# Squares of the late tiles on ScalarE, in their own PSUM banks, and their sums on VectorE one tile later

## The chip, the cores and the metric

The kernel runs on one core of a Trainium2 chip. Such a core has five engines that work side by side, each through its own queue in a fixed order: TensorE (PE in the rows; its weight loads are PEld) multiplies matrices into PSUM, VectorE (DVE), ScalarE (ACT) and GpSimd (POOL) work element by element, and SyncE (SP) issues most DMA transfers. Engines wait for one another only through semaphores. The metric is the device time in microseconds (us) of one execution of the whole program; lower is better. TensorE's clock is granted by the chip at one of two levels, 2.4 or 1.2 GHz; the profile shows it as 1.0 or 0.5.

## The reference, cut to what matters

Two layers of a diffusion backbone on 512 latent tokens, with 256 context tokens beside them in the first layer. The model width is 1024.

```
for i in range(2):
    h = modulate(rmsnorm(x, g_mix_pre), shift, scale)
    y = token_mixer(h) @ w_out                     # "output product"
    x = x + gate * rmsnorm(y, g_mix_post)          # "residual"
    h = modulate(rmsnorm(x, g_ffn_pre), shift, scale)
    a, u = split(h @ w_ffn_in)
    y = (silu(a) * u) @ w_ffn_out                  # "hidden product"
    x = x + gate * rmsnorm(y, g_ffn_post)
```

`rmsnorm(y, g)` is `y * rsqrt(mean(y*y) + eps) * g`, with the mean over the 1024 features of a token. So after each product y the kernel needs the sum of the squares of all eight tiles of y before it can form a residual, and then the sum of squares of the new x before it can form the next h.

## The kernel before, in words

**Layout and stages.** Everything is stored feature-major: 128 features on the partitions, 8 tiles of features (`KT`), tokens along the free axis. An output tile m is a chain of matmuls over 8 feature tiles (6 for the last block of the hidden product). Each fp32 product is made of three reduced-precision matmuls (weight high x activation high, high x low, low x high), so a tile takes 24 (or 18) matmuls. Weights stream from memory in chunks: SyncE loads a chunk into `raw` (two places), ScalarE rounds it to `w_hi` (line 1304), GpSimd forms `w_lo` (line 913), and TensorE uses it from a ring of four places (`RING`). A load waits until GpSimd is done with the chunk two before it; a rounding waits until TensorE has used the chunk four before it.

**The order.** `build_order` writes out by hand one list of units of work, `ORDER`. Every engine walks through the same list and issues its own share of each unit, so the list fixes each queue.

**The transitions.** Between a product y and the next stage lies a transition, written by `tail(L, w)`: L is the layer, w = 0 after the output product and w = 1 after the hidden product. There are four. The tokens are cut into two parts: in layer 0 columns 0 to 511 (latent) and 512 to 767 (context), in layer 1 two halves of 256. Product tiles of the first part are done before the transition. In it, TensorE makes the second part's tiles, the eight units `late(m)` for m = 0 to 7, each of 256 columns, in bank 1 of the PSUM tensor `A[m % 2]`, while the first part goes through `mean` (a matmul with 1/1024 that sums the squares over partitions; line 1268), `res` (residual, VectorE, lines 2052 and 2053 or 2060 and 2061), `sq` (squares of x on ScalarE, line 1613, summed by TensorE, line 1277), `rstd` (ScalarE, lines 1317 to 1321) and `nrm` (norm and modulation: VectorE line 2071, ScalarE lines 1621, 1624, 1627, VectorE line 2078 for four of the eight tiles and GpSimd line 958 for the others). Between the late tiles stand `modk` units, products for the next modulation (line 995); SyncE loads a later piece of their weights only when an earlier one has been used, and weight chunks queue behind that load.

The order of a transition in layer 0: late 0, mean 0, late 1, take 0, res 0 and 1, take 1; then four times late(2+i), ahead(1+i), squares of x, a modulation product, two residuals (not the fourth time), take(2+i); then rstd, late 6, ahead 5, nrm 0 to 2, late 7, ahead 6, take 6, nrm 3 to 7, ahead 7, take 7, head 0 of the first part, mean 1 of the second part, then the second part's res, sq, rstd and nrm. Layer 1's first transition is alike. Its last one has no squares of x and no norms: late(2+i), two residuals, take(2+i), and at the end late 6, take 6, late 7, take 7, mean 1.

**`take(m)`** evicts late tile m (VectorE, lines 1972 to 1989). With w = 0 it copies the tile to y, squares it into a spare bank of `N` and adds the square to the running sum `ssq`; with w = 1, y already holds the sum of the earlier blocks, so it adds the tile to y, squares and adds. The semaphore `free[A0]` or `free[A1]` goes up when the second of these instructions (the first with w = 1) is done; `late(m+2)` waits for it at `unit_free`.

**`head(L, w, 0, 0)`** is the first tile of the next stage's product for the first part. It is made in A0: before its first matmul TensorE waits until all earlier users of A0, late(6) among them, have been evicted (lines 1027 to 1032), then before each of the eight k-steps for the normalised tile k. `mean(L, w, 1)` stands behind it in TensorE's queue.

**`ahead(j)`** is a weight rounding on ScalarE (`high`), and `link` makes an engine wait for its own last instruction.

Of the kernel before, what the change touches and what calls it, by code (L numbers as in the profile page):

```python
# [12 lines left out]
ACT = mybir.ActivationFunctionType  # L13

P = 128
DEPTH, D, SEQ, CTX = 2, 1024, 512, 256
# [311 lines left out]
def sums_before(L, w):  # L328

    return KT * (4 * L + 2 * w)  # L330
# [88 lines left out]
LOW_V = (0, 3, 5, 7)  # L419
SQ, NRM, RES = ({e: i + 1 for i, e in enumerate(x for x in ORDER if x[0] == kind)} for kind in ("sq", "nrm", "res"))  # L420
# [62 lines left out]
def bass_hybrid_block(nc: bass.Bass, stream, pairs, modw, xT, pos_row, pos_col, cols, wdec, masks, mats, wide, x_keep, out):  # L483
    with ExitStack() as ctx:
# [3 lines left out]
        def sem(name):  # L488
            return ctx.enter_context(nc.semaphore(name))
# [134 lines left out]
        haff_ready, hhi_ready = sem("haff_ready"), sem("hhi_ready")  # L624
        yn_ready, rstd_copied, half_done = sem("yn_ready"), sem("rstd_copied"), sem("half_done")
# [67 lines left out]
        def rstd_at(e):  # L693

            t0, t1, _ = span(e)
            return sum_bank(e) if e in IN_PSUM else rstd[:, t0:t1]

# [266 lines left out]
        def _(pe):  # L964
# [35 lines left out]
            for e in ORDER:  # L1000
# [263 lines left out]
                elif kind == "mean":  # L1264
                    unit_free(e)
                    t0, t1, _ = span(e)
                    pe.wait_ge(ssq_ready, sums_before(L, e[2]) + KT * (e[3] + 1))
# [13 lines left out]
        def _(act):  # L1281
# [112 lines left out]
            for e in ORDER:  # L1394
# [200 lines left out]
                elif kind == "ahead":  # L1595
                    high(TWICE[0] + KT + e[3] if L else PLAN.n0[("late",) + e[1:]] + RING)
                elif kind == "mean":
# [51 lines left out]
        def _(dve):  # L1649
# [131 lines left out]
            for e in ORDER:  # L1781
# [190 lines left out]
                elif kind == "take":  # L1972
                    w, m = e[2:]
                    t0, t1, _ = parts(e)[1]
                    late = ("late", L, w, m)
                    at = t0 + L * SEQ // 2
                    ym, src = y[:, m, t0:t1], A[m % 2][:, at:at + t1 - t0]
                    dve.wait_ge(chunk_used, (TWICE[w] + m if L else PLAN.n0[late]) + 1)
                    square = N[:, 512:512 + t1 - t0]
                    if w:  # L1980
                        dve.tensor_tensor(ym, src, ym, ALU.add).then_inc(free[f"A{m % 2}"], 1)
                        read_out(dve, late)
                        link(dve.tensor_tensor(square, ym, ym, ALU.mult))
                    else:
                        link(dve.tensor_copy(ym, src))
                        dve.tensor_tensor(square, src, ym, ALU.mult).then_inc(free[f"A{m % 2}"], 1)
                        read_out(dve, late)
                    dve.wait_ge(ssq_ready, sums_before(L, w) + KT + m)
                    dve.tensor_tensor(ssq[:, t0:t1], square, ssq[:, t0:t1], ALU.add).then_inc(ssq_ready, 1)
# [220 lines left out]
```

## Time and profile before

| | |
|---|---|
| device time, median of 3 runs | 1675.63 us (1671.38 to 1683.51) |
| profiled execution | 1675.34 us, span 1673.5 us |
| busy in the span | TensorE 95%, VectorE 44%, ScalarE 34%, GpSimd 36% |
| mean granted clock | 0.988 |
| DMA | 111 GB/s mean |
| first transition (about 386 to 446 us) | TensorE busy 54.8 of 60 us |
| second (940 to 1012) | 59.6 of 72 |
| third (1244 to 1312) | 59.9 of 68 |
| last (1643 to 1673.5) | 19.1 of 30.5 |

A line "L975 PE MATMUL A<-h_hi,w_hi" names the line of the kernel, the engine, the operation, the tile written and the tiles read (buffer numbers left out). Times of a timeline count from the start of the span. The bracket at the end of a row says how long the engine had been idle and whose work ended that wait.

### The profile page before, as it was taken

To read this page: it belongs to the slowest core of one execution; us is meant where nothing else is said; L and a number is where in the kernel's file an instruction comes from. 1 tells how busy PE (TensorE), PEld (TensorE's weight loads), DVE (VectorE), ACT (ScalarE), POOL (GpSimd) and SP (SyncE) were. 2 spreads that over 40 slices of the span, in tenths; PEclk is the share of its full clock that TensorE was granted. 3 is DMA by queue.
4 is the path that set the end of the run, shared out by engine and by line. 5 is a ranking of instruction groups with operands and counts; after the bars stand their busy time and mean duration, and the time that the engine had idled before them with its cause. 6 is when DMAs were issued, how large, how long until landed. Compare 5 with 4: busy or idle time off the path is not lost.

```text
span 1673.5 us, 23315 instructions
## 1 busy us (share of the span) xinstructions
PE 1596.0 (95%) x9320; PEld 1347.2 (81%) x9320; DVE 728.7 (44%) x1208; ACT 573.7 (34%) x924; POOL 603.2 (36%) x317
## 2 busy tenths in 40 slices
PE   5999999999899999999999989999989999999997
PEld 2778877877689989998998657887886888888887
DVE  2400325845666425761465554045754321221137
ACT  4534213524634313441243345432523422222221
POOL 1422211334424425553255433232132444444442
PEclk9999999999999999999999999999999999999999
DMA  9444332154312112222123653211071222222221
GB/s 374 160 160 151 124 107 80 39 201 176 151 39 93 72 38 83 69 77 75 51 76 117 261 195 107 66 67 59 28 277 51 79 97 100 89 100 92 97 87 64
DMA packets 50210, 185.25 MB, mean 111 GB/s; under 512 B 5254, under 2 KB 10246, under 8 KB 43208
## 3 DMA queue, kind: packets, MB, share of 16 engines
q1 hardware_dynamic: 44028, 170.29, 28.1%
q10 hardware_dynamic: 6092, 13.70, 2.2%
q8 instruction: 64, 1.05, 0.2%
q14 instruction: 26, 0.21, 0.0%
HBM read 172.44 MB, written 11.53 MB: 110 GB/s over the span
## 4 chain that ended last, share of the span: by engine, by line
PE 81%; DVE 5%; issue 4%; DMA 3%; ACT 3%; POOL 3%; SPq 1%; ACTq 0%; DVEq 0%; POOLq 0%
PE A L975 55%; PE A L1221 7%; PE N L1221 4%; PE G L1221 4%; DMA raw<-stream 2%; POOL w_lo L913 2%; PE G L1277 1%; DMA raw<-modw 1%; PE N L995 1%; PE G L995 1%; PE A L1117 1%; PE G L1083 1%; PE G L1051 1%; PE N L1067 1%; PE G L1124 1%
## 5 line engine op out<-in xcount | busy, mean ns | idle before, releaser
L913 POOL TENSOR_TENSOR w_lo<-raw,w_hi 128x1024 fp32r<-128x1024 f32 (+2 forms) x175 | 403.2, 2307 | 729.1 <-ACT w_hi L1304 692.3
L975 PE MATMUL A<-h_hi,w_hi 128*128 128x512 f32 (+1 forms) x1264 | 416.4, 360 | 21.8 <-POOL h_lo L958 12.7
L975 PE MATMUL A<-h_hi,w_lo 128*128 128x512 f32 (+1 forms) x1264 | 407.1, 353 | 0.0
L975 PE MATMUL A<-h_lo,w_hi 128*128 128x512 f32 (+1 forms) x1264 | 406.5, 352 | 0.0
L1304 ACT ACTIVATE w_hi<-raw 128x1024 fp32r<-128x1024 f32 (+2 forms) x175 | 177.2, 1015 | 429.2 <-PE A L975 362.5
L975 PEld LDWEIGHTS A<-h_hi,w_hi 128*128 128x128 f32 x1264 | 223.4, 190 | 80.7 <-POOL h_lo L958 18.8
L975 PEld LDWEIGHTS A<-h_hi,w_lo 128*128 128x128 f32 x1264 | 224.1, 191 | 33.0
L975 PEld LDWEIGHTS A<-h_lo,w_hi 128*128 128x128 f32 x1264 | 223.8, 191 | 31.9 <-issue 0.5
L975 PE MATMUL A<-g_hi,w_hi 128*128 128x512 f32 (+1 forms) x528 | 165.2, 352 | 3.8 <-DVE g_lo L1778 2.0
L975 PE MATMUL A<-g_lo,w_hi 128*128 128x512 f32 (+1 forms) x528 | 162.9, 348 | 0.0
L975 PE MATMUL A<-g_hi,w_lo 128*128 128x512 f32 (+1 forms) x528 | 162.9, 348 | 0.0
L953 POOL TENSOR_TENSOR w_lo<-w_sum,w_hi 128x512 fp32r<-128x512 f32 x45 | 81.0, 1824 | 146.4 <-DVE w_sum L1705 100.0
L1836 DVE TENSOR_TENSOR eu<-eu,ktok 128x256 f32<-128x256 f32 x24 | 34.4, 1434 | 186.0 <-ACT dec L1450 185.9
L975 PEld LDWEIGHTS A<-g_hi,w_hi 128*128 128x128 f32 x528 | 90.9, 189 | 23.4 <-issue 5.2
L975 PEld LDWEIGHTS A<-g_lo,w_hi 128*128 128x128 f32 x528 | 90.6, 188 | 15.0 <-issue 1.0
L975 PEld LDWEIGHTS A<-g_hi,w_lo 128*128 128x128 f32 x528 | 90.7, 188 | 14.1
L1337 ACT ACTIVATE w_hi<-w_sum 128x512 fp32r<-128x512 f32 x81 | 49.2, 625 | 120.8 <-DVE w_sum L1705 120.8
L2029 DVE TENSOR_TENSOR sqb<-sqb,A 128x512 f32<-128x512 f32 x22 | 15.1, 688 | 147.5 <-PE A L975 147.5
L2032 DVE TENSOR_TENSOR g_lo<-sqb,g_hi 128x512 f32 (+1 forms) x22 | 50.7, 2305 | 24.0 <-ACT g_hi L1567 24.0
L958 POOL TENSOR_TENSOR h_lo<-y,h_hi 128x256 fp32r<-128x256 f32 (+1 forms) x32 | 31.5, 989 | 78.8 <-ACT h_hi L1624 78.4
L1277 PE MATMUL G<-sqs,one_d 128*128 128x512 f32 (+1 forms) x80 | 35.3, 571 | 22.0 <-ACT sqs L1613 21.8
L953 POOL TENSOR_TENSOR w_lo<-raw,w_hi 128x512 fp32r<-128x512 f32 x27 | 39.0, 1458 | 31.0 <-ACT w_hi L1337 31.0
(294 smaller groups left out, 2494.0 us busy)
## 6 DMA issues: line engine op xcount, KB each, us to landing
raw<-stream SPq DMA_DIRECT2D x150, 512.0 KB, 3.2
mraw<-modw SPq DMA_DIRECT2D x38, 1024.0 KB, 5.0
raw<-pairs SPq DMA_DIRECT2D x18, 512.0 KB, 4.6
raw<-stream SPq DMA_DIRECT2D x24, 384.0 KB, 2.9
raw<-modw SPq DMA_DIRECT2D x6, 1024.0 KB, 14.7
x<-x_keep ACTq DMA_DIRECT2D x4, 1536.0 KB, 11.0
mraw<-pairs SPq DMA_DIRECT2D x9, 512.0 KB, 3.2
x_keep<-x SPq DMA_DIRECT2D x4, 768.0 KB, 21.6
```

The source lines that it names most:

```text
L913: pool.tensor_tensor(lo, like_chunk(n, raw[:, n % RAW, 0:WIDTH[n]]), hi.bitcast(F32), ALU.subtract).then_inc(lo_done, 1)
L953: pool.tensor_tensor(lo, src, f_weight(w_hi, q, pos).bitcast(F32), ALU.subtract).then_inc(f_lo, 1)
L958: pool.tensor_tensor(h_lo[:, k, t0:t1], y[:, k, t0:t1], h_hi[:, k, t0:t1].bitcast(F32), ALU.subtract).then_inc(hlo_ready_p, 1)
L975: m = pe.matmul(dst[:, t0:t1], a, b[:, k, t0:t1], start=(first and p == 0), stop=(last and p == 2))
L995: mm = pe.matmul(dst[32 * j:32 * j + 32, 0:512], csil[:, k, :], piece_at(p)[:, 512 * j:512 * j + 512], start=(k == 0), stop=(k == KT - 1))
L1051: pe.matmul(unit_of(e), lrT[0:33, tt * P:(tt + 1) * P], wd[:, :], start=True, stop=True).then_inc(full["z"], 1)
L1221: m = pe.matmul(dst, a[:, cols], b[:, k, :], start=(k == 0 and p == 0), stop=(k == 3 and p == 2))
L1277: pe.matmul(sum_bank(e), one_d[:, :], sq_at(e), start=(k == 0), stop=(k == KT - 1)).then_inc(sq_used, 1)
L1304: act.activation(w_hi[:, n % RING, 0:width], src, ACT.Copy).then_inc(hi_done, 1)
L1337: act.activation(f_weight(w_hi, q, pos), src, ACT.Copy).then_inc(f_hi, 1)
L1836: dve.tensor_tensor(eu[:, g, :], eu[:, g, :], ktok[:, tt, :], ALU.mult).then_inc(ku_ready, 1)
L2032: dve.tensor_tensor(g_lo[:, gp, 0:T], sqb[:, 0:1, 0:T], g_hi[:, gp, 0:T].bitcast(F32), ALU.subtract).then_inc(g_ready, 1)
```

## The change

ScalarE now has a share in every `take`. With w = 0 it copies the late tile from PSUM to y, waits for that, and squares the tile in place, in its PSUM bank. With w = 1 VectorE still adds the tile to y, and ScalarE then writes the square of y into the tile's PSUM bank. VectorE adds a square to `ssq` one unit later: in take(m) it adds the square of tile m-1 straight from the bank, in take(7) those of 6 and 7. Only that addition raises `free[A0]` or `free[A1]`. The second part's `mean` waits for the releases of tiles 6 and 7. The order list is unchanged.

```diff
--- before.py
+++ after.py
@@ -327,7 +327,7 @@
 
 def sums_before(L, w):
 
-    return KT * (4 * L + 2 * w)
+    return KT * (2 * L + w)
 
 
 def span(e):
@@ -417,6 +417,8 @@
 PIECE = {e: i for i, e in enumerate(PIECES)}
 MTURN = {e: i + 1 for i, e in enumerate(x for x in ORDER if x[0] == "mturn")}
 LOW_V = (0, 3, 5, 7)
+TAKE = {e: i + 1 for i, e in enumerate(x for x in ORDER if x[0] == "take")}
+ADDED = {e: i + 1 for i, e in enumerate(x for x in ORDER if x[0] == "take" and x[2])}
 SQ, NRM, RES = ({e: i + 1 for i, e in enumerate(x for x in ORDER if x[0] == kind)} for kind in ("sq", "nrm", "res"))
 
 YN = {e: i + 1 for i, e in enumerate(x for x in ORDER if x[:4] == ("res", 1, 1, 1) and x[4] % 2)}
@@ -622,6 +624,7 @@
         ssq_ready, rstd_ready, xnew_ready, sq_ready, sq_used = (
             sem("ssq_ready"), sem("rstd_ready"), sem("xnew_ready"), sem("sq_ready"), sem("sq_used"))
         haff_ready, hhi_ready = sem("haff_ready"), sem("hhi_ready")
+        late_added, late_sq = sem("late_added"), sem("late_sq")
         yn_ready, rstd_copied, half_done = sem("yn_ready"), sem("rstd_copied"), sem("half_done")
         hlo_ready_p, hlo_ready_v = sem("hlo_ready_p"), sem("hlo_ready_v")
         pair_in, sums_ready, f_hi, f_lo, f_used = (
@@ -694,6 +697,16 @@
 
             t0, t1, _ = span(e)
             return sum_bank(e) if e in IN_PSUM else rstd[:, t0:t1]
+
+        def late_at(e):
+
+            t0, t1, _ = parts(e)[1]
+            at = t0 + e[1] * SEQ // 2
+            return A[e[3] % 2][:, at:at + t1 - t0]
+
+        def late_done(e):
+
+            return (TWICE[e[2]] + e[3] if e[1] else PLAN.n0[("late",) + e[1:]]) + 1
 
         def sq_at(e):
 
@@ -1264,7 +1277,11 @@
                 elif kind == "mean":
                     unit_free(e)
                     t0, t1, _ = span(e)
-                    pe.wait_ge(ssq_ready, sums_before(L, e[2]) + KT * (e[3] + 1))
+                    if e[3]:
+                        for m in (KT - 2, KT - 1):
+                            read_out(pe, ("late", L, e[2], m))
+                    else:
+                        pe.wait_ge(ssq_ready, sums_before(L, e[2]) + KT)
                     pe.matmul(sum_bank(e), one_d[:, :], ssq[:, t0:t1],
                               start=True, stop=True).then_inc(full["mean"], 1)
                 elif kind == "sq":
@@ -1594,6 +1611,16 @@
                             high(n0 + j + RING, i, width=WIDTH[n0] if e[2] == 2 else None)
                 elif kind == "ahead":
                     high(TWICE[0] + KT + e[3] if L else PLAN.n0[("late",) + e[1:]] + RING)
+                elif kind == "take":
+                    t0, t1, _ = parts(e)[1]
+                    ym = y[:, e[3], t0:t1]
+                    if e[2]:
+                        act.wait_ge(late_added, ADDED[e])
+                        act.activation(late_at(e), ym, ACT.Square).then_inc(late_sq, 1)
+                    else:
+                        act.wait_ge(chunk_used, late_done(e))
+                        link(act.activation(ym, late_at(e), ACT.Copy))
+                        act.activation(late_at(e), ym, ACT.Square).then_inc(late_sq, 1)
                 elif kind == "mean":
                     if e[2] and e[3] == 0:
                         act.preload_act_table_set(LN_SET)
@@ -1972,21 +1999,15 @@
                 elif kind == "take":
                     w, m = e[2:]
                     t0, t1, _ = parts(e)[1]
-                    late = ("late", L, w, m)
-                    at = t0 + L * SEQ // 2
-                    ym, src = y[:, m, t0:t1], A[m % 2][:, at:at + t1 - t0]
-                    dve.wait_ge(chunk_used, (TWICE[w] + m if L else PLAN.n0[late]) + 1)
-                    square = N[:, 512:512 + t1 - t0]
                     if w:
-                        dve.tensor_tensor(ym, src, ym, ALU.add).then_inc(free[f"A{m % 2}"], 1)
-                        read_out(dve, late)
-                        link(dve.tensor_tensor(square, ym, ym, ALU.mult))
-                    else:
-                        link(dve.tensor_copy(ym, src))
-                        dve.tensor_tensor(square, src, ym, ALU.mult).then_inc(free[f"A{m % 2}"], 1)
-                        read_out(dve, late)
-                    dve.wait_ge(ssq_ready, sums_before(L, w) + KT + m)
-                    dve.tensor_tensor(ssq[:, t0:t1], square, ssq[:, t0:t1], ALU.add).then_inc(ssq_ready, 1)
+                        dve.wait_ge(chunk_used, late_done(e))
+                        dve.tensor_tensor(y[:, m, t0:t1], late_at(e), y[:, m, t0:t1], ALU.add).then_inc(late_added, 1)
+                    for j in ((m - 1,) if 0 < m < KT - 1 else (m - 1, m) if m else ()):
+                        of = e[:3] + (j,)
+                        dve.wait_ge(late_sq, TAKE[of])
+                        if j:
+                            read_out(dve, ("late", L, w, j - 1))
+                        dve.tensor_tensor(ssq[:, t0:t1], late_at(of), ssq[:, t0:t1], ALU.add).then_inc(free[f"A{j % 2}"], 1)
                 elif kind == "ffn_in" and L == 0:
                     for q in range(FAST):
                         if q == 3:
```

## Rows read from the trace of the kernel before

**Rows 1.** The page's first part: busy us (share of the span) xinstructions.

```profile
PE 1596.0 (95%) x9320; PEld 1347.2 (81%) x9320; DVE 728.7 (44%) x1208; ACT 573.7 (34%) x924; POOL 603.2 (36%) x317
```

**Rows 2.** Eviction lines: xcount, duration ns min/median/max, first and last start, form.

```profile
L1981 DVE TENSOR_TENSOR y<-A,y x16: 414/416/426, 948.7 to 1662.7; 128x256 f32<-128x256 f32 x16
...
L1985 DVE COPY y<-A x16: 414/422/425, 388.6 to 1287.3; 128x256 f32<-128x256 f32 x16
...
L1986 DVE TENSOR_TENSOR N<-A,y x16: 432/432/433, 389.1 to 1287.7; 128x256 f32<-128x256 f32 x16
...
L1989 DVE TENSOR_TENSOR sqb<-N,sqb x32: 424/424/425, 389.6 to 1663.6; 128x256 f32<-128x256 f32 x32
```

**Rows 3.** TensorE's waits, whole span: us in total, times, longest us.

```profile
PE G L1277 <- ACT sqs L1613: 21.8, 6, 12.4
...
PE N L1268 <- DVE sqb L1989: 2.6, 3, 1.5
...
PE A L975 <- DVE y L1981: 1.2, 2, 0.7
```

**Rows 4.** ScalarE, PSUM to SBUF and to PSUM (columns as rows 2).

```profile
L1319 ACT ACTIVATE rstd<-N,eps x5: 474/474/476, 30.0 to 1004.1; 128x256 f32<-128x256 f32 x5
...
L1321 ACT ACTIVATE N<-N x5: 368/368/582, 390.1 to 1646.6; 128x256 f32<-128x256 f32 x3, 128x512 f32<-128x512 f32 x2
```

**Rows 5.** TensorE's timeline (start, us), first transition: late(2), head, second mean begin.

```profile
392.09 0.28 PE L975 MATMUL A<-h_hi,w_hi 128*128 128x256 f32 x1
...
421.03 0.50 PE L975 MATMUL A<-h_hi,w_hi 128*128 128x512 f32 x1
...
430.74 0.67 PE L1268 MATMUL N<-sqb,one_d 128*128 128x256 f32 x2 [0.41 <-DVE sqb L1989]
```

**Rows 6.** VectorE's timeline, first transition: take(1) and take(7) begin.

```profile
393.58 0.41 DVE L1985 COPY y<-A 128x256 f32<-128x256 f32 x1
...
429.25 0.42 DVE L1985 COPY y<-A 128x256 f32<-128x256 f32 x1
```

**Rows 7.** Chain of waits (start, us, what), first transition: an unstalled head.

```profile
432.41 5.71 PE A L975 x24
```

**Rows 8.** TensorE's timeline, second transition: two square products, and the second mean.

```profile
956.24 1.10 PE L1277 MATMUL G<-sqs,one_d 128*128 128x512 f32 x2 [2.63 <-ACT sqs L1613]
...
959.92 1.99 PE L1277 MATMUL G<-sqs,one_d 128*128 128x512 f32 x4 [0.47 <-ACT sqs L1613]
...
992.51 0.59 PE L1268 MATMUL N<-sqb,one_d 128*128 128x256 f32 x2
```

**Rows 9.** VectorE's timeline, second transition: take(1) and take(7) begin.

```profile
954.87 0.41 DVE L1981 TENSOR_TENSOR y<-A,y 128x256 f32<-128x256 f32 x1
...
989.26 0.42 DVE L1981 TENSOR_TENSOR y<-A,y 128x256 f32<-128x256 f32 x1
```

**Rows 10.** The chain of waits, last transition: late 6 and 7, and the mean.

```profile
1658.05 4.59 PE A L975 x36
...
1664.17 0.68 PE N L1268 x2
```

**Rows 11.** ScalarE's timeline, third transition: a weight rounding, and norm 3.

```profile
1253.66 1.06 ACT L1304 ACTIVATE w_hi<-raw 128x1024 fp32r<-128x1024 f32 x1 [5.98 <-DMA raw<-stream]
...
1283.52 0.48 ACT L1621 ACTIVATE h_hi<-A,coef 128x256 fp32r<-128x256 f32 x1 [0.70 <-DVE A L2071]
```

**Rows 12.** Timeline, third transition: take(7) begins; the second mean.

```profile
1287.30 0.42 DVE L1985 COPY y<-A 128x256 f32<-128x256 f32 x1
...
1288.79 0.67 PE L1268 MATMUL N<-sqb,one_d 128*128 128x256 f32 x2 [0.66 <-DVE sqb L1989]
```

**Rows 13.** VectorE's timeline, last transition: take(1)'s first instruction.

```profile
1648.69 0.41 DVE L1981 TENSOR_TENSOR y<-A,y 128x256 f32<-128x256 f32 x1
```

**Rows 14.** The chain of waits, second transition: the end of the head.

```profile
988.07 4.60 PE A L975 x12
```

**Rows 15.** That stretch: us, busy PE PEld DVE ACT POOL (x), clock, DMA, GB/s.

```profile
988.10:991.60 3.50, 3.50 (x10) 2.72 (x11) 1.96 (x6) 1.50 (x2) 1.15 (x1) 0.59 0.54 152
```

## The prediction, written before the change was run

> **What bounds the kernel now.** The page's busy times come first: TensorE is busy 95% of the span [rows 1], so only its idle time, or new idle time, can move the result. Which idle time touches this change is seen in the waits of TensorE and in the rows of the eviction lines. The 32 late evictions cost VectorE three instructions each, 0.42 to 0.43 us apiece [rows 2], but TensorE waited for them for only 2.6 us before the mean products and 1.2 us at bank releases [rows 3]. About 4 us is all that a quicker eviction could return there. The larger waits (21.8 us for ScalarE's squares of x) belong to a chain that the change does not shorten. The next views are the timelines of the four transitions. The reader should see what TensorE does while the chain residual, square, rstd, norm runs on VectorE and ScalarE: it works on late tiles and then on the next stage's first product ("head"), whose eight steps take each normalised tile as it appears.
>
> **What is removed and added.** In an output-product transition (w = 0) VectorE loses the copy and the square and keeps the addition; ScalarE gets a copy and a square. In a hidden-product transition (w = 1) VectorE keeps y+A and the addition, and ScalarE gets the square. The nearest rows for ScalarE on 256 columns are 0.47 us (Ln, PSUM to SBUF) and 0.37 us (Exp, PSUM to PSUM) [rows 4]. I take 0.47 for the copy and 0.42 for the square, 0.9 for the pair; ends 0.7 and 1.0.
> The Trainium skill's page VectorE: DVE Perf Modes, section on the TRN2 errata, gives ScalarE 172 cycles plus the column count at 1.2 GHz for PSUM to SBUF, so 0.36 us for the copy, an estimate; the sum would be 0.1 us shorter, and rows 4 say it is too low.
>
> **What is moved** is what counts: the release of bank A(m). Before, it followed take(m)'s second instruction (first where w = 1). After, it follows the addition inside take(m+1), and for m = 6 and 7 both inside take(7). All waits for that release stay where they were: late(m+2) on TensorE, and the head, which waits until late(6) has left A0. VectorE's queue order is fixed, so everything that stands there between take(m) and take(m+1) now lies ahead of the release: two residual pairs for late(2), norms 0 to 2 for late(7), norms 3 to 7 for the head. ScalarE's weight roundings, squares of x and norms queue behind its new instructions. SyncE and GpSimd get nothing new; their loads are late only where TensorE's modulation products are, because SyncE waits for those.
>
> *Layer 0, output product.* Late(2) started at 392.09 us, while VectorE finished the residuals only when the old take(1) could start, 393.58 [rows 5, 6]. The addition (0.42) takes that place, so late(2) starts at 394.1: 2.0 us late. TensorE has no slack before the squares of x, so rstd and the norms are 2.0 late. ScalarE, which sets the pace of norms 3 to 7, gets take(6)'s pair between norms 2 and 3: another 0.9. VectorE therefore reaches take(7) at 429.25 + 2.9 = 432.15 instead of 429.25 [rows 6] and releases A0 at 432.6. The head, which began at 421.03 and ran under the norms [rows 5], can start only at 432.7. It needs the 5.71 us that the next, unstalled head of 24 matmuls took [rows 7]: end 438.4. The mean product behind it started at 430.74 [rows 5]: **+7.7 us**. The late(7) stall (it waits for norms 0 to 2) and the last square are hidden inside this wait. All that follows hangs on that mean, so it moves by as much.
>
> *Layer 0, hidden product.* Y+A of take(1) starts at 954.87 [rows 9], the addition ends 0.8 later, and late(2) runs from 955.8 to 958.1 (36 such matmuls took 4.59 us, half of that for 18 [rows 10]). TensorE's first square product started at 956.24, after an idle 2.63, and a later one after an idle 0.47 [rows 8]. So 1.9 us is lost and 0.5 absorbed: 1.4. ScalarE's extra square in take(6): 0.4. VectorE reaches take(7) at 989.26 + 1.8 = 991.1 [rows 9], needs y+A and the addition (0.84), and the head runs from 992.0 to 997.8. The mean started at 992.51 [rows 8]: **+5.3 us**.
>
> *Layer 1, output product.* Late(2) is some 0.5 late (it waits for one residual pair of 256 columns), but the square of x waits for ScalarE, which sits out 5.98 us for a weight load [rows 11]: absorbed, cost nothing; were that load early, it would be 0.5. ScalarE's pair fits in its idle 0.70 but for 0.2 [rows 11]. Take(7) is reached at 1287.30 + 0.2 [rows 12], the release comes 0.42 later, the head takes 24/36 of 4.59 = 3.06 [rows 10] and ends at 1291.1, where the mean started at 1288.79 [rows 12]: **+2.3 us**.
>
> *Layer 1, hidden product.* Here nothing but residuals lies between late tiles. Take(2+i) first waits for late(2+i), then adds, and only then frees the bank for late(3+i): the two banks become one. Each tile costs 2.3 us of matmuls, two VectorE instructions of 0.42 and the hand-overs, 3.2 us together. Late(2) starts 0.9 after take(1) at 1648.69 [rows 13], five more follow, and late(7) ends at 1649.6 + 5 x 3.2 + 2.3 = 1667.9, against 1662.6 before (1658.05 + 4.59) [rows 10]. The last square takes as long as VectorE's did, and VectorE loses one instruction: **+5.0 us** on the mean at 1664.17 [rows 10].
>
> The four make **20.3 us**.
>
> *Clock.* Where TensorE had stood idle inside the second transition's head, the granted clock fell: a mean of 0.59 over 988.10 to 991.60, between the levels 2.4 and 1.2 GHz, and 12 matmuls took 4.60 us [rows 14, 15], against 12/24 of 5.71 = 2.86 [rows 7]: 1.7 us lost. The change puts idle times of 7, 5 and 3 us right ahead of three heads. I charge 1.7 each: **+5.1**. Ends: 0, and seven such losses (12) if the last transition's repeated 0.9 us gaps count too.
>
> **Sum.** 20.3 + 5.1 = 25.4 on the profiled execution's own 1675.34 us (span 1673.5 and 1.8 around it) gives 1700.7. That execution lies 0.3 below the median 1675.63 of the three runs, which spread from 1671.38 to 1683.51. I forecast **1701 us**; its own range is 1694 to 1708.
>
> **Rivals.**
> *Clock worse.* TensorE's own rows after idle time speak for it [rows 14, 15]; against it, part of the lowered stretch falls into the idle time itself. 20.3 + 12 and some: 1709. Chance 0.13.
> *The heads are covered.* If the release on which the head waits came early (norms not ahead of it on VectorE, or ScalarE no longer the pace), only the late(2) stalls and the last transition would stay: 2.0 + 0.9, 1.8, 0.2 and 5.0, about 10: 1686. The fixed order speaks against it. Chance 0.12.
> *Not slower: the freed VectorE decides.* Place: VectorE between rstd and the head. Price: 3.8 us of TensorE's waits [rows 3] and two instructions (0.85) less in the norms of three transitions, 2.5: 6.3 together, so 1669. It decides only if each bank comes free before TensorE asks for it, that is if VectorE passes its norms before late(7) ends; it passed them at 429.25 while the head, behind late(7), began at 421.03 [rows 5, 6]. The Trainium skill's page TensorEngine Tiling (Array Packing), section PSUM Bottleneck, advises using both ScalarE and VectorE to evacuate PSUM; that is this rival, and the time it would give is the one just worked out. Chance 0.06.
> *The change does not spread the work.* ScalarE's takes block its own queue: it waits for late(m), or for VectorE's addition, ahead of the weight roundings. If one weight tile in each of the first three transitions came 3 us late to TensorE, 1701 + 9 = 1710. Roundings run four tiles ahead, which speaks against it. Chance 0.05.
> The forecast keeps 0.64.
>
> **How the numbers follow.** A difference of 1% (17 us) is about what separates a change from none for this kernel. The forecast, the worse clock and the blocked queue lie above it: 0.82, of which I move 0.01 to same for the nearness of 1694. The covered heads and the freed VectorE lie within it, 0.18, of which 0.03 is kept for a faster result than any case explains. Slower 0.81, same 0.16, faster 0.03. The range 1688 to 1712 takes in the clock's lower end (1695.6), a weight load in the second transition that does not shift (1.4 less), the spread of runs, and the upper rivals; 1686 and below stay out.
>
> **What would show it.** In the changed kernel's profile TensorE should have a new wait for VectorE's additions of squares of about 6 us ahead of the first head, 5 ahead of the second and 2 to 3 ahead of the third; waits of 0.9 us five or six times in the last transition; and a late(2) that starts as the second residual ends. VectorE's busy time should fall by about 32 x 0.43 = 14 us and ScalarE's rise by 16 x 0.9 + 16 x 0.4 = 21. Heads that still start under the norms, or late tiles that run back to back in the last transition, would prove the prediction wrong.

## The result, and the profile after

The changed kernel took 1705.11 us (median of 4 runs, 1694.80 to 1709.43) against 1674.68 us before (4 runs, 1671.38 to 1683.51): a ratio on record of 1.0154, interval 1.0125 to 1.0183 (the bare quotient of these two medians is 1.018, at the upper end of it). The forecast was 1701, the range 1688 to 1712. The profiled execution of the changed kernel is its quickest run (1694.8, span 1693.0), so its trace has 19.5 us to explain; the other 10 up to the median are taken up under "Clock" below.

The first part of the page of the changed kernel, busy us (share of the span) xinstructions:

```profile
PE 1595.7 (94%) x9320; PEld 1349.6 (80%) x9320; DVE 711.1 (42%) x1160; ACT 589.5 (35%) x972; POOL 603.0 (36%) x317
```

TensorE did the same work as in [rows 1]; VectorE shed 17.6 us and ScalarE took on 15.8. The work moved as intended, and the kernel is slower: TensorE is busy as long as before, so in sum the loss of this execution is idle time of TensorE. Its waits over the whole span of the changed kernel (us in total, times, longest us), which answer to [rows 3]:

```profile
PE A L988 <- DVE sqb L2010: 30.8, 14, 6.6
PE G L1294 <- ACT sqs L1640: 17.5, 4, 12.9
...
PE N L1285 <- DVE sqb L2010: 2.3, 1, 2.3
```

L2010 is VectorE's addition of a square, which now releases the bank. A wait that the kernel before did not have holds 30.8 us. The wait for ScalarE's squares of x shrank by 4.3 us; the second transition shows where it went: before, TensorE idled 2.63, 0.47 and 3.13 us there for squares of x, after the change only 2.72, with 3.69 spent ahead of late(2).

Where these 14 waits stand is seen in the distance from the first mean product to the second in each of the four transitions, in us (begin to begin, profiled executions; L0 and L1 are the layers, w0 the output product, w1 the hidden product):

| | L0 w0 | L0 w1 | L1 w0 | L1 w1 | sum |
|---|---|---|---|---|---|
| before | 42.38 | 44.04 | 42.58 | 18.73 | 147.7 |
| after | 52.01 | 48.05 | 42.51 | 24.82 | 167.4 |
| difference | +9.6 | +4.0 | -0.1 | +6.1 | +19.7 |
| predicted, without clock | +7.7 | +5.3 | +2.3 | +5.0 | +20.3 |

The transitions hold 19.7 us, so the stretches outside them, which differ by -1.6 to +1.2 us each, come to -0.2 together. The 14 waits divide as follows: late(2), late(7) and the head in each of the first two transitions (10.9 and 11.0 us), late(2) and late(7) in the third (3.4), and six late tiles in the last (5.6). The head of the third transition is not among them.

**First transition.** TensorE's timeline of the changed kernel at late(2), at late(7), and at the head with the second mean (start us, us, work, count, idle before it and who ended that):

```profile
395.24 0.38 PE L988 MATMUL A<-h_hi,w_hi 128*128 128x256 f32 x1 [1.83 <-DVE sqb L2010]
...
422.92 0.39 PE L988 MATMUL A<-h_hi,w_hi 128*128 128x256 f32 x1 [2.46 <-DVE sqb L2010]
...
433.66 0.80 PE L988 MATMUL A<-h_hi,w_hi 128*128 128x512 f32 x1 [6.62 <-DVE sqb L2010]
434.26 0.63 PE L988 MATMUL A<-h_lo,w_hi 128*128 128x512 f32 x1
...
438.78 0.39 PE L988 MATMUL A<-h_hi,w_hi 128*128 128x512 f32 x1
...
441.53 0.59 PE L1285 MATMUL N<-sqb,one_d 128*128 128x256 f32 x2
```

Late(2) begins 5.7 us after the first mean, where the kernel before had 3.7 ([rows 5]; its first mean began at 388.36): 2.0 us later, behind two residual pairs. The head, which used to begin at 421.03 and to run under the norms, waits 6.62 us for the addition of tile 6. VectorE's timeline at the same place shows what stood ahead of that addition, and the second release right behind ScalarE's pair:

```profile
432.50 0.75 DVE L2099 SCALAR_TENSOR_TENSOR h_lo<-A,coef,h_hi 128x512 fp32r<-128x512 f32 x1 [1.40 <-ACT y L1654]
433.19 0.42 DVE L2010 TENSOR_TENSOR sqb<-A,sqb 128x256 f32<-128x256 f32 x1
...
434.96 0.42 DVE L2010 TENSOR_TENSOR sqb<-A,sqb 128x256 f32<-128x256 f32 x1 [1.35 <-ACT A L1623]
```

The last norm is the instruction ahead of it. Tile 6 had left TensorE long before; its bank was held by the queue, not by the work on it. Then the head itself ran slowly. The windows of this head, of the second transition's head, and of the idle time ahead of the first (us; busy PE, PEld, DVE, ACT, POOL with counts; granted clock; DMA share; GB/s):

```profile
433.70:441.50 7.80, 7.80 (x24) 6.25 (x25) 0.42 (x1) 1.19 (x3) 0.00 (x0) 0.69 0.01 3
1000.10:1005.70 5.60, 5.59 (x25) 4.63 (x26) 0.42 (x1) 1.33 (x2) 0.00 (x0) 1.00 0.56 230
427.10:433.60 6.50, 0.00 (x0) 0.00 (x0) 4.35 (x9) 5.10 (x9) 3.10 (x3) 0.86 0.83 316
```

24 matmuls of the same shape took 7.87 us (433.66 to 441.53) at a mean clock of 0.69, and 5.57 (1000.11 to 1005.68) at 1.00. The clock had already begun to fall within the idle time (0.86). The rows at 0.63 us are those at 1.2 GHz, the rows at 0.39 those at 2.4.

**Last transition.** TensorE's timeline of the changed kernel at late(3), late(7) and the mean:

```profile
1665.98 0.39 PE L988 MATMUL A<-g_hi,w_hi 128*128 128x256 f32 x1 [0.85 <-DVE sqb L2010]
...
1678.89 0.39 PE L988 MATMUL A<-g_hi,y_ctx 128*128 128x256 f32 x1 [0.85 <-DVE sqb L2010]
...
1683.60 0.67 PE L1285 MATMUL N<-sqb,one_d 128*128 128x256 f32 x2 [2.29 <-DVE sqb L2010]
```

That is a tile every 3.2 us, each behind a wait of 0.85 from late(3) on (1.32 ahead of late(2)), as the two banks work like one. The 2.29 us ahead of the mean is longer than a square and an addition need. ScalarE's timeline there:

```profile
1678.54 0.39 ACT L1619 ACTIVATE A<-y 128x256 f32<-128x256 f32 x1 [2.87 <-DVE y L2004]
1678.54 4.02 ACTq L1670 DMA_DIRECT2D out_dram<-x  x8
1682.61 0.39 ACT L1619 ACTIVATE A<-y 128x256 f32<-128x256 f32 x1 [3.68 <-DVE y L2004]
```

Eight output DMAs, issued by ScalarE between its squares of tiles 6 and 7, fill its queue up to 1682.56. Tile 7 was there for the square at about 1681.7. The row's bracket names VectorE's y+A, but that had ended; the ACTq row shows the true releaser.

### The profile page after: what moved, and what is told of

Its sections match the earlier page's. It is cut to its first block, busy times and chain, and to the rows that moved or that the text cites. A ratio compares the mean times of both kernels' runs of the same rounds, so it can differ in the third digit from the quotient of the medians.

```text
span 1693.0 us, 23309 instructions
## 1 busy us (share of the span) xinstructions
PE 1595.7 (94%) x9320; PEld 1349.6 (80%) x9320; DVE 711.1 (42%) x1160; ACT 589.5 (35%) x972; POOL 603.0 (36%) x317
## 4 chain that ended last, share of the span: by engine, by line
PE 81%; issue 4%; DVE 4%; ACT 3%; DMA 3%; POOL 3%; SPq 1%; ACTq 0%; POOLq 0%; DVEq 0%
PE A L988 56%; PE A L1234 7%; PE N L1234 4%; PE G L1234 4%; POOL w_lo L926 2%; DMA raw<-stream 2%; DMA raw<-modw 1%; PE G L1294 1%; PE N L1008 1%; PE A L1130 1%; PE G L1008 1%; PE G L1096 1%; SPq L855 1%; PE G L1064 1%; PE N L1080 1%
## 5 line engine op out<-in xcount | busy, mean ns | idle before, releaser
L988 PE MATMUL A<-h_hi,w_hi 128*128 128x512 f32 (+1 forms) x1264 | 415.3, 359 | 30.5 <-DVE sqb L2010 14.8
L988 PEld LDWEIGHTS A<-h_hi,w_hi 128*128 128x128 f32 x1264 | 223.0, 190 | 86.5 <-DVE sqb L2010 17.5
L988 PE MATMUL A<-g_hi,w_hi 128*128 128x512 f32 (+1 forms) x528 | 166.4, 354 | 13.4 <-DVE sqb L2010 9.6
L1294 PE MATMUL G<-sqs,one_d 128*128 128x512 f32 (+1 forms) x80 | 34.2, 557 | 17.6 <-ACT sqs L1640 17.5
## 6 DMA issues: line engine op xcount, KB each, us to landing
x<-x_keep ACTq DMA_DIRECT2D x4, 1536.0 KB, 10.7
```

Of the source, the lines that this page charges most:

```text
L988: m = pe.matmul(dst[:, t0:t1], a, b[:, k, t0:t1], start=(first and p == 0), stop=(last and p == 2))
L1294: pe.matmul(sum_bank(e), one_d[:, :], sq_at(e), start=(k == 0), stop=(k == KT - 1)).then_inc(sq_used, 1)
```

## The experiments

Theory A: the release of a bank waits in VectorE's in-order queue (held banks). Rival B: ScalarE's extra instructions delay the chain of the norms. Each distance comes from one profiled execution. The experiments ran in two groups with medians of the kernel before of 1678.50 us (13 runs) and 1676.04 us (23 runs). The distances of the transitions, in the same order as above:

| kernel | L0 w0 | L0 w1 | L1 w0 | L1 w1 | median us | ratio [interval] |
|---|---|---|---|---|---|---|
| the change again | 51.89 | 51.30 | 44.19 | 24.75 | 1703.90 | 1.0141 [1.0108, 1.0174] |
| early release | 43.08 | 42.29 | 40.51 | 18.83 | 1676.97 | 0.9984 [0.9968, 1.0000] |
| VectorE holds | 54.59 | 51.44 | 44.34 | 27.09 | 1713.18 | 1.0206 [1.0162, 1.0250] |
| tile 6 in take(6) | 47.87 | 49.57 | 42.30 | 24.75 | 1694.57 | 1.0085 [1.0053, 1.0117] |
| change, sends spread | 51.97 | 53.67 | 42.91 | 23.97 | 1704.12 | one run |
| early, sends spread | 43.09 | 44.66 | 42.21 | 17.03 | 1674.81 | 0.9990 [0.9974, 1.0006] |
| change, idle filled | 49.75 | 50.59 | 43.19 | 24.76 | 1702.87 | 1.0159 [1.0131, 1.0187] |
| early, VectorE copies | 42.65 | 45.24 | 41.87 | 17.03 | 1676.62 | 1.0000 [0.9984, 1.0017] |

**The change again** (no edit).

> The changed kernel again, unaltered, for a second profile and more times. Its profiled execution was 1694.8 us at a mean granted clock of 0.987, three others 1703 to 1709 at 0.979 to 0.981. Theory 'held banks': the distances from first to second mean product stay at 52.0, 48.1, 42.5 and 24.8 us (before: 42.4, 44.0, 42.6, 18.7) up to 2 to 3 us of clock. Theory 'clock': the executions above 1700 owe 8 to 15 us to more stretches at the lower level, somewhere; a second profile above 1700 would show where. Median expected 1703.

The loss repeats. The first and the last transition repeat to 0.1 us; those in the middle do not (+3.3 and +1.7).

**Early release.** The same division of work, but the square goes to a buffer of its own in SBUF, and whoever reads the product last frees the bank at once:

```diff
-                    if e[2]:
-                        act.wait_ge(late_added, ADDED[e])
-                        act.activation(late_at(e), ym, ACT.Square).then_inc(late_sq, 1)
-                    else:
+                    if not e[2]:
                         act.wait_ge(chunk_used, late_done(e))
-                        link(act.activation(ym, late_at(e), ACT.Copy))
-                        act.activation(late_at(e), ym, ACT.Square).then_inc(late_sq, 1)
+                        act.activation(ym, late_at(e), ACT.Copy).then_inc(free[f"A{e[3] % 2}"], 1)
+                    read_out(act, ("late",) + e[1:])
+                    if e[3] > 1:
+                        act.wait_ge(late_sum, TAKE[e] - 2)
+                    act.activation(late_square(e), ym, ACT.Square).then_inc(late_sq, 1)
...
-                        dve.tensor_tensor(y[:, m, t0:t1], late_at(e), y[:, m, t0:t1], ALU.add).then_inc(late_added, 1)
+                        dve.tensor_tensor(y[:, m, t0:t1], late_at(e), y[:, m, t0:t1], ALU.add).then_inc(free[f"A{m % 2}"], 1)
...
-                        dve.tensor_tensor(ssq[:, t0:t1], late_at(of), ssq[:, t0:t1], ALU.add).then_inc(free[f"A{j % 2}"], 1)
+                        dve.tensor_tensor(ssq[:, t0:t1], late_square(of), ssq[:, t0:t1], ALU.add).then_inc(late_sum, 1)
```

> As the changed kernel, with the same work on ScalarE, but the square goes to SBUF (two places of 256 columns in sqs) and the bank is released as soon as the tile is in y (by ScalarE's copy with w = 0, by VectorE's y+A with w = 1). VectorE still adds one tile later. Held banks: back to before, distances about 43, 44.5, 42.5 and 17.5 to 18.5 us, the whole 1672 to 1678. Rival 'ScalarE's extra work in the norm chain or its blocked queue': stays near 52, 48, 42.5, 25 and 1700. Rival 'VectorE's relief': 1669 or less.

The whole loss is gone: 1676.97 us, 0.9984 of the kernel before, though ScalarE and VectorE run as many instructions as in the changed kernel; only the place of the square differs. The page:

```profile
PE 1593.6 (95%) x9320; PEld 1346.9 (81%) x9320; DVE 718.3 (43%) x1160; ACT 589.8 (35%) x972; POOL 606.5 (36%) x317
```

ScalarE's 589.8 is that of the changed kernel (589.5). So B is refuted as the cause; its place is the 0.7 us by which the first transition is longer than before. What the division of work can gain is seen here too: the interval allows 0.3% at most. Two things changed at once, the release and the place of the square, so this run alone does not tell them apart; "Tile 6 in take(6)" below leaves the square in the bank and moves one release. Three distances missed the expectation. The second and the third came 2.2 and 2.0 us under it; it had been taken from the one profiled execution of the kernel before, whose granted clock over these transitions was 0.92 and 0.96, against 0.96 and 1.00 here. The last took 18.83, above the 17.5 to 18.5 expected. ScalarE's timeline of this kernel shows why, and TensorE's mean behind it:

```profile
1656.52 3.85 ACTq L1673 DMA_DIRECT2D out_dram<-x  x8
1660.47 0.42 ACT L1626 ACTIVATE sqs<-y 128x256 f32<-128x256 f32 x1 [3.54 <-issue]
```

```profile
1661.49 0.67 PE L1288 MATMUL N<-sqb,one_d 128*128 128x256 f32 x2 [3.31 <-DVE sqb L2013]
```

The late tiles end 3.3 us ahead of the mean; the eight DMA issues hold the last square.

**VectorE holds.** The opposite: VectorE does all three instructions again, as before the change, but the square stays in the bank and the release stays one tile late:

```diff
...
-    link(act.activation(ym, late_at(e), ACT.Copy))
-    act.activation(late_at(e), ym, ACT.Square).then_inc(late_sq, 1)
...
+    dve.wait_ge(chunk_used, late_done(e))
+    if w:
+        link(dve.tensor_tensor(ym, late_at(e), ym, ALU.add))
+        dve.tensor_tensor(late_at(e), ym, ym, ALU.mult).then_inc(late_sq, 1)
+    else:
+        link(dve.tensor_copy(ym, late_at(e)))
+        dve.tensor_tensor(late_at(e), late_at(e), ym, ALU.mult).then_inc(late_sq, 1)
```

> VectorE does all three instructions again as before (copy or y+A, square, addition) and ScalarE none, but the square lies in the tile's own bank and the addition with the release comes one tile later, as in the changed kernel. Held banks: as slow as the changed kernel or slower, since two or three VectorE instructions now stand before each release: distances about 53, 49, 44 and 27.5 us (last transition: 2.3 + 3 x 0.42 + 0.1 = 3.7 per tile), the whole about 1700 to 1708. Rival 'ScalarE's extra work': equal to before, 1675.

1713.18 us, with none of this work on ScalarE: the late release makes the loss without it. TensorE's waits for the additions that release the banks are 38.0 us, against 30.8 in the changed kernel. The four distances came within 1.6, 2.4, 0.3 and 0.4 us of the expected ones; the median lies above the expectation, with a granted clock of 0.973 to 0.980 in its four runs against 0.982 to 0.989 in runs of the kernel before. With the same held banks, ScalarE's share in the changed kernel makes the transitions shorter (172.1 and 167.4 us in sum against 177.5): spreading the work does help, once the banks are held.

**Tile 6 in take(6).** The addition and the release of tile 6 come right behind its square, ahead of norms 3 to 7:

```diff
- for j in ((m - 1,) if 0 < m < KT - 1 else (m - 1, m) if m else ()):
+ for j in ((m,) if m == KT - 1 else (m - 1, m) if m == KT - 2 else (m - 1,) if m else ()):
```

> The changed kernel, but the square of tile 6 is added (and A0 released) in take(6), ahead of norms 3 to 7, instead of in take(7). Held banks: the head runs under the norms again, though VectorE waits in take(6) for ScalarE's square, some 1.2 us into the norms; distances 46, 45, 40.5 us, and about 26 in the last transition, where take(6) must wait for its own square (0.5). The whole 8 to 11 us under the changed kernel. Rival 'late(2) and late(7) carry the loss, not the head': the distances stay within 1 us of the changed kernel's.

1694.57 us, 9.3 under the change measured beside it (1703.90). The first transition fell from 52.0 to 47.9. TensorE's timeline there has the head under the norms again:

```profile
434.54 0.51 PE L988 MATMUL A<-h_hi,w_hi 128*128 128x512 f32 x1 [0.81 <-POOL h_lo L971]
...
436.93 0.67 PE L1285 MATMUL N<-sqb,one_d 128*128 128x256 f32 x2 [0.37 <-DVE sqb L2010]
```

So a bank that still holds its square costs less as soon as its release stands ahead of the norms. Not all of the 9.3 us is shown to be that: the four distances come to 164.5 us, 7.6 less than in the repeated change and only 2.9 less than in the first profiled execution of the change, and the repeated one also carries a stretch at the lower clock ahead of the first transition (see "Clock"). The first three distances came 1.8 to 4.6 us above what was expected. VectorE waited 2.76 us in take(6) of the first transition for ScalarE's pair (until 426.66), where 1.2 was expected, with norms 3 to 7 behind it; and late(7) still waits for norms 0 to 2 (2.45 us of TensorE there, 3.52 in the second transition). The last transition (24.75, no head in it) did not change, where 26 was expected: VectorE's addition of tile 6 in take(6) (by 1680.2) lies beside late(7)'s matmuls.

**Sends spread, on the change and on the early release.** The eight output DMAs of the first half (the sends) are issued behind the squares of tiles 2 to 6, as the residuals come ready:

```diff
+ if e[1:3] == (1, 1) and e[3] > 1:
+     u0, u1, _ = parts(("res", 1, 1))[0]
+     for k in {2: (0, 1), 3: (2, 3), 4: (4, 5), 5: (6,), 6: (7,), 7: ()}[e[3]]:
+         act.wait_ge(xnew_ready, KT + RES[("res", 1, 1, 0, k)])
+         act.dma_start(out[:, k:k + 1, u0:u1], x[:, k:k + 1, u0:u1]).then_inc(out_sent, 16)
...
- for k in ((0, 2, 4, 6, 1, 3, 5, 7) if s else range(KT)):
+ for k in ((0, 2, 4, 6, 1, 3, 5, 7) if s else ()):
```

> The change, with the eight output DMAs of the first half taken out of ScalarE's queue behind the take of tile 6 and issued behind the takes of tiles 2 to 6 instead, as the residuals come ready. Theory (the sends stood ahead of the last square, which started about 0.8 us after its tile was copied out): the last transition goes from 24.8 us to 24.0 to 24.4 us between its two means. Rival (the last square waited for its tile alone, and the sends cost nothing): 24.7 to 24.9 us. The other three transitions do not change.

> The kernel that releases the banks early, with the eight output DMAs of the first half issued behind the takes of tiles 2 to 6. Theory (in that kernel the late tiles end 3.3 us ahead of the second mean, because ScalarE is still issuing the DMAs): the last transition goes from 18.8 us to 16.9 to 17.4 us, the whole kernel 1.5 to 2 us under the early release, so 0.997 to 0.998 of the kernel before. Rival (the last transition is bound by something else on ScalarE or VectorE): 18.5 to 18.9 us and 0.998 to 1.000.

The last transition fell from 24.8 to 23.97 and from 18.83 to 17.03 us: the sends cost 0.8 us in the changed kernel and 1.8 in the early release. (The first of the two kernels was run once; its second transition took 53.67, so not every other transition stayed as expected.) The mean's wait in the early release with spread sends:

```profile
1665.63 0.67 PE L1288 MATMUL N<-sqb,one_d 128*128 128x256 f32 x2 [1.52 <-DVE sqb L2018]
```

1.52 us in place of 3.31. The whole kernel at 0.9990 [0.9974, 1.0006] cannot be told from the one before: 1.7 us won in the last transition, 0.1% of the time, is less than the width of this interval. The expected 0.997 to 0.998 is not shown.

**Idle time filled.** 54 and 27 products that nobody reads stand ahead of the first and the second head, into a free half of N:

```diff
+ if (L, j, s) == (0, 0, 0):
+     f0, f1, _ = parts(("late", 0, w, 0))[1]
+     for _ in range((54, 27)[w]):
+         pe.matmul(N[:, 512:512 + f1 - f0], h_hi[:, 0, f0:f0 + P], h_hi[:, 0, f0:f1], start=True, stop=True)
```

> The change, with products that nobody reads put into TensorE's idle time ahead of the first and the second head (54 and 27 of 128x256, into a free half of the bank N), about 5.8 and 2.9 us of work in waits of 6.6 and 3.6 us. Theory (the idle time costs twice: the wait itself, and then the head's products at the lower of the two clock levels): the first head takes 5.6 us in place of 7.9, and the first transition goes from 52.0 to 49.5 to 50.3 us; the second head ran at full clock already, 47.5 to 48.5 us. Rival (the head's clock falls for another reason than the idle time before it): the first transition stays at 51.5 to 52.5 us.

TensorE's timeline of the first transition in this kernel:

```profile
427.36 6.73 PE L1041 MATMUL N<-h_hi 128*128 128x256 f32 x54
434.05 0.50 PE L988 MATMUL A<-h_hi,w_hi 128*128 128x512 f32 x1
...
439.64 0.59 PE L1289 MATMUL N<-sqb,one_d 128*128 128x256 f32 x2
```

```profile
434.10:439.60 5.50, 5.50 (x24) 4.56 (x25) 0.42 (x1) 1.21 (x3) 0.00 (x0) 1.00 0.02 7
```

The head took 5.59 us at a clock of 1.00, against 7.87 at 0.69: what the idle time took a second time was 2.3 us, and the transition fell by as much, to 49.75. But the second transition came to 50.59, not to the expected 47.5 to 48.5, with its head at 5.57 us. The same transition of the change took 48.05 and 51.30 us in two executions, and the expectation stood on the shorter. The kernel as a whole, 1702.87 us, cannot be told from the change (1703.90 and 1705.11): 2.3 us are 0.14%, and the intervals are some 0.3% wide to each side. So the filler shows that the clock at this head depends on what TensorE did before it; it neither shows nor excludes a gain of that size in the whole.

**Early release, VectorE copies tiles 6 and 7 of the first transition.**

Against the early release with the sends spread:

```diff
- if not e[2]:
+ if not e[2] and not (e[1] == 0 and e[3] > 5):
...
+ if L == 0 and w == 0 and m > 5:
+     dve.wait_ge(chunk_used, late_done(e))
+     dve.tensor_copy(y[:, m, t0:t1], late_at(e)).then_inc(free[f"A{m % 2}"], 1)
```

> The early release with the spread sends, and in the first transition VectorE, not ScalarE, takes tiles 6 and 7 out of their banks; ScalarE still squares them. Theory (the 0.7 us that early release loses in the first transition is ScalarE's pair for tile 6 in the chain of the norms): the first transition goes from 43.1 to 42.5 to 42.8 us, and the kernel stands at 0.996 to 0.998 of the kernel before. Rival (it is ScalarE's rounding of a weight, or something else): 43.0 to 43.3 us.

42.65 against 43.09: of the 0.7 us over the kernel before, 0.4 was ScalarE's copy in the chain of the norms, by one profile of each. The kernel as a whole, 1.0000 [0.9984, 1.0017], shows nothing of it, and the expected 0.996 to 0.998 was missed. No version here beats the kernel before by more than can be measured.

## Why the prediction was right

**The mechanism** (the release moves behind everything that stands in VectorE's queue between take(m) and take(m+1)) is shown from both sides: without the late release the loss is gone (0.9984), and with the late release but VectorE's old work it is 2.06%. The closeness of the sum in the first profiled execution (20.3 without the clock predicted, 19.7 with it measured) is partly luck: the four misses, +1.9, -1.3, -2.4 and +1.1 us, nearly cancel.

**Layer 0, output product, +7.7 predicted, +9.6 measured.** Late(2) was 2.0 late and the head began once the norms were through, both as predicted. The head began 44.1 us after the first mean, where the prediction's numbers give 44.3, and took 7.87 us, where 5.71 was put in: 7.7 - 0.2 + 2.2 = 9.7. The 2.2 is the clock, for which 1.7 was charged in its own term.

**ScalarE's pair.** Of the changed kernel, the copy and the square of the output product (duration min/median/max):

```profile
L1622 ACT ACTIVATE y<-A x16: 361/380/383, 392.7 to 1298.1; 128x256 f32<-128x256 f32 x16
```

```profile
L1623 ACT ACTIVATE A<-y x16: 387/388/390, 393.1 to 1298.5; 128x256 f32<-128x256 f32 x16
```

0.77 us together, inside the ends 0.7 and 1.0, where 0.9 was taken. The prediction held the estimate of 0.36 us for the copy too low on account of [rows 4]; the row just shown has 0.38, so the nearest row (a Ln at 0.47) was the worse guide. The Trainium skill's page VectorE: DVE Perf Modes, section on the TRN2 errata, from which that 0.36 was an estimate, agrees with this row to 0.02 us.

**Busy times.** The prediction expected VectorE to shed 14 us, from 32 instructions. By its own account of what is removed it is 48: two in each of 16 takes and one in each of the other 16 (the counts of the page fell from 1208 to 1160). VectorE shed 17.6 us, and ScalarE took on 15.8 where 21 was expected. Neither number enters the forecast.

**Layer 0, hidden product, +5.3 predicted, +4.0 measured.** The waits came, but in other sizes: late(2) waited 3.69 us, late(7) 3.70, the head 3.56, where about 5 was expected at the head. The wait of late(7), which the prediction did not count here, took its share. The head began 42.5 us after the first mean, where the prediction's numbers give 43.5, and ran at full speed. This transition differs most between executions: 48.05, 51.30 and, with only the sends of the last transition moved, 53.67 after the change, against 44.04 in the one profile before it. So neither the single 4.0 nor a mean over the three (51.0, 7.0 above before) tests the 5.3.

**Layer 1, output product, +2.3 predicted, -0.1 measured.** Two things were wrong here. The first is the start: late(3) began 10.7 us after the first mean, before 13.0. TensorE's rows of the two kernels at the first square of x (first before, then after), and the window of each:

```profile
1255.17 1.19 PE L1277 MATMUL G<-sqs,one_d 128*128 128x256 f32 x2 [2.63 <-ACT sqs L1613]
1256.29 2.95 PE L995 MATMUL G<-two_low,csil 128*32 128x512 f32 x16
```

```profile
1267.08 0.67 PE L1294 MATMUL G<-sqs,one_d 128*128 128x256 f32 x2 [1.35 <-ACT sqs L1640]
1267.68 1.92 PE L1008 MATMUL G<-two_low,csil 128*32 128x512 f32 x16
```

```profile
1255.10:1259.20 4.10, 4.03 (x19) 1.13 (x19) 0.59 (x2) 1.69 (x3) 4.10 (x2) 0.60 0.19 62
```

```profile
1267.00:1270.00 3.00, 2.92 (x22) 1.18 (x23) 1.36 (x4) 2.18 (x5) 3.00 (x2) 1.00 0.03 5
```

The clock stood at 0.60 before and at 1.00 after, worth 1.55 us in these two rows, and ScalarE's weight load came 0.7 us earlier after the mean. So the failing step is the use of one execution's clock as if it were fixed: the kernel before had low stretches here that a later transition need not have. The second is the place of the wait. From late(3) to the second mean the changed kernel took 31.8 us, 2.2 more than before, but not by the 2 to 3 us ahead of the head that were predicted. TensorE's rows at late(7) and at the head, and the window of late(7):

```profile
1292.59 0.58 PE L988 MATMUL A<-h_hi,y_ctx 128*128 128x256 f32 x1 [3.06 <-DVE sqb L2010]
...
1298.04 0.58 PE L988 MATMUL A<-h_hi,w_hi 128*128 128x256 f32 x1
```

```profile
1291.90:1298.20 6.30, 5.62 (x25) 5.36 (x25) 4.39 (x13) 4.92 (x13) 2.93 (x4) 0.50 0.00 0
```

TensorE waited 3.06 us ahead of late(7), for which the prediction had no term here, and then made late(7) at clock 0.50. By its end the bank had been released, and the head began without a wait. In the repeated change late(7) ran at full speed, and the head did wait, 2.36 us, as predicted; the transition took 44.19 there, +1.6. So the low clock cost little at this place: what it added to late(7) went out of the head's wait.

**Layer 1, hidden product, +5.0 predicted, +6.1 measured.** 3.2 us for a tile was right. What was missing was the eight sends on ScalarE, 0.8 us of the 1.1. The prediction asked of each wait what is queued behind it, but did not ask what is queued ahead of ScalarE's new last square.

**Clock, +5.1 charged.** The charge was 1.7 us at each of three heads. The first profiled execution shows it at the first head only (7.87 us); the second ran at full clock, and in the third transition 1.55 us was given back. In the repeated change all three heads ran slow. TensorE's rows at the start of its second and its third head:

```profile
1006.49 0.79 PE L988 MATMUL A<-h_hi,w_hi 128*128 128x512 f32 x1 [3.48 <-DVE sqb L2010]
...
1307.08 0.58 PE L988 MATMUL A<-h_hi,w_hi 128*128 128x256 f32 x1 [2.36 <-DVE sqb L2010]
```

From start to the mean behind them the three heads took 7.74, 7.12 and 4.31 us (the last two mean products began at 1013.61 and 1311.39), against 5.57, 5.57 and the prediction's 3.06: 5.0 us in all, as charged. The four distances of that execution come to 172.1 us, 24.4 above before, where 20.3 + 5.1 = 25.4 was predicted. So the clock term holds for one execution and not for the other. What it left out lies ahead of the transitions. The repeated change has its profile at the level of its median (1705.81; span 1704.0). Its window of a stretch ahead of the first transition, then that of the profiled execution of the changed kernel:

```profile
334.00:347.40 13.40, 12.70 (x68) 8.60 (x67) 4.11 (x11) 3.14 (x5) 1.40 (x1) 0.50 0.04 6
```

```profile
334.00:347.40 13.40, 12.09 (x89) 8.57 (x88) 6.39 (x15) 4.49 (x8) 2.37 (x1) 1.00 0.32 117
```

Clock 0.50 for 13.4 us against 1.00, in code that the change does not touch; the first mean came at 394.3 us instead of 389.5. In all, the lowered stretches of that trace last 68 us, those of the profiled execution of the change 45, of the kernel before 42. 23 us more at half speed would be about 11 us, which is the distance between the two executions (1704.0 and 1693.0). By place it is 4.8 us up to the first mean, 4.7 in the four transitions and 1.5 in the rest. Against the kernel before, the repeated change is 30.5 us longer in its span: 24.4 in the transitions and 6.0 ahead of the first mean. So the rival "clock worse" has part of the truth: three of the four runs of the change had a granted clock of 0.979 to 0.981 and took 1703 to 1709 us. The whole loss, clock included, is gone with the early release (ten runs, 0.985 to 0.989), but whether the held banks bring about the stretch at 334 us, which lies ahead of them, is not shown. Why it appears in some executions and not in others is open; the kernel before was profiled once.

**The rivals.** Heads covered (1686): no, waits of 6.62 and 3.56 us stood ahead of the first two; the third alone was covered in the profiled execution. Freed VectorE decides (1669): no; the early release shows what it is worth once a bank comes free with its last reader, near to this rival's condition (2.4 us of TensorE's waits for the evictions are left), and it is 0.9984, not 0.996. The Trainium skill's page TensorEngine Tiling (Array Packing), section PSUM Bottleneck, gives its advice for the case that tiling has made TensorE faster and the copy out of PSUM may have become the bottleneck. Here it was not: TensorE waited only some 4 us for evictions [rows 3], and sharing them brought nothing that these runs can tell from zero. A blocked ScalarE queue (1710): the profiled execution has two waits for weights that the kernel before had not (1.8 us, ahead of the third transition); "VectorE holds" has them too (1.6) with none of this work on ScalarE, and the repeated change has none, so they do not come from this queue.

## What to carry to other kernels

A PSUM bank is free when its releasing instruction has run, not when its data has been used: put the release on the last reader, and never behind work of the next stage in an in-order queue. When you move work to a lightly loaded engine, list what that queue holds ahead of the new instruction as well as behind it, DMA issues included. Cost an idle gap ahead of dense matmuls once for itself and once for the clock, and take the second part from more than one execution: in one execution 3.56 us of idle time was followed by a head of 5.57 us, in another 3.48 us by one of 7.12.

## What the hardware showed that was not expected

Issuing a DMA from ScalarE took its queue for 0.34 to 0.47 us each (eight in 4.02 us), as much as a 128x256 activation (0.37 to 0.42 us); two banks and a short square do not help if eight of these stand in between. And TensorE's clock differed more between two executions of the same code (45 and 68 us at the lower level, some 11 us of time) than the prediction charged for the heads (5.1). Keeping TensorE busy through one gap gave back the 2.3 us at that gap; in the time of the whole kernel so little could not be seen.
